# Output projection without a staged operand, TensorE's tiles written out, and zero rows stored early: one change to a one-core decoder step

## The reference, cut to what matters

```python
mixed = jnp.concatenate([y_rwkv, y_gmlp, y_sb], axis=-1) @ lw['w_out']
x = x + gate1 * mixed
h2 = rms_norm(x, lw['norm2_g']) * (1.0 + scale2) + shift2
moe = hier_moe(h2.reshape(B * T, D_MODEL), ...)   # top-1 group of 4, then top-2 of its 4 experts
x = x + gate2 * moe
```

## Time and profile before

| | us |
|---|---|
| median of 3 runs | 1441.96 |
| lowest and highest of the 3 | 1438.92, 1447.1 |
| the profiled execution, its own time | 1445.0 |
| its span, first to last instruction | 1443.4 |
| TensorE busy in the span | 1245.0 (86%) |
| VectorE, ScalarE, GpSimd busy | 594.9, 412.9, 174.6 |
| `out_project`, TensorE's first to last product | 912.1 to 1043.8 |
| `experts`, TensorE's first gate_up to its last matmul | 1098.7 to 1375.6 |
| `combine`, first matmul to the end | 1391.9 to 1443.4 |

### The profile page before, as it was taken

The page is one execution under the profiler, slowest core; times in us unless marked ns, Lnnn a source line. Parts: engine busy times, 40 slices in busy tenths (PEclk is TensorE's granted clock), DMA queues, the critical chain, the costliest instruction groups (busy, mean ns, idle before and its releaser), DMA issues. The chain is left out here.

```text
span 1443.4 us, 29072 instructions
## 1 busy us (share of the span) xinstructions
PE 1245.0 (86%) x10925; PEld 769.6 (53%) x10925; DVE 594.9 (41%) x1007; ACT 412.9 (29%) x850; POOL 174.6 (12%) x380
## 2 busy tenths in 40 slices
PE   5899989999976888999889987799926999999955
PEld 2465466565644565554569887344414555555421
DVE  3300514464555554466235556223371222222227
ACT  3100205565665563431112322012110111111113
POOL 0100101112121442000000000400001110011040
PEclk9899989999998899999989999799957999999978
DMA  9300305101000894247321000710107679856875
GB/s 359 115 0 0 112 15 161 41 5 46 17 1 17 309 404 129 71 138 258 91 104 18 4 4 3 219 70 30 44 8 287 208 251 349 294 164 231 296 264 179
DMA packets 88554, 191.78 MB, mean 133 GB/s; under 512 B 18523, under 2 KB 41570, under 8 KB 83203
## 3 DMA queue, kind: packets, MB, share of 16 engines
q1 hardware_dynamic: 70244, 142.36, 28.7%
q0 software_dynamic: 11056, 36.45, 7.2%
q10 hardware_dynamic: 7152, 11.55, 2.5%
HBM read 163.01 MB, written 27.31 MB: 132 GB/s over the span
## 5 line engine op out<-in xcount | busy, mean ns | idle before, releaser
L2660 PE MATMUL ex_ps_g<-all_mT,ex_xt 128*64 128x256 f32 x1344 | 156.2, 385 | 4.6 <-DMA all_mT<-in_exp_wu 3.2
L2270 PE MATMUL op_ps_o<-all_hT,op_m_t 128*128 128x512 f32 x256 | 115.7, 608 | 7.8 <-POOL op_m_t L2250 7.8
L2660 PEld LDWEIGHTS ex_ps_g<-all_mT,ex_xt 128*64 128x64 f32 x1344 | 93.7, 138 | 53.7 <-DMA all_mT<-in_exp_wu 4.8
L583 PE MATMUL rp_ps<-all_hT,kv_rp_w 128*128 128x384 f32 (+1 forms) x336 | 107.0, 473 | 0.8 <-PEq L1932 0.8
L352 PE MATMUL fr_big<-all_mT,all_hT 128*128 128x256 f32 (+3 forms) x288 | 95.7, 496 | 3.0 <-DVE all_hT L405 3.0
L1707 PE MATMUL at_ps_p<-all_hT,mix_at_w 128*128 128x363 f32 (+1 forms) x288 | 96.0, 476 | 0.0
L1862 DVE TENSOR_TENSOR_SCAN mix_v_g<-mix_v_g 128x1024 f32<-128x1024 f32 (+3 forms) x32 | 46.8, 1485 | 102.1 <-ACT at_A L1814 72.8
L583 PEld LDWEIGHTS rp_ps<-all_hT,kv_rp_w 128*128 128x128 f32 x336 | 62.5, 190 | 46.5 <-issue 10.9
L2679 PE MATMUL ex_ps_y<-all_hT,ex_hid_T 128*64 128x512 f32 x336 | 80.4, 599 | 4.3 <-DMA all_hT<-in_exp_wd 1.9
L2270 PEld LDWEIGHTS op_ps_o<-all_hT,op_m_t 128*128 128x128 f32 x256 | 48.5, 194 | 66.1 <-issue 57.9
L352 PEld LDWEIGHTS fr_big<-all_mT,all_hT 128*128 128x128 f32 (+1 forms) x288 | 54.6, 190 | 43.5 <-issue 38.2
(11 more groups left out here) (470 smaller groups left out, 2066.7 us busy)
## 6 DMA issues: line engine op xcount, KB each, us to landing
all_mT<-in_exp_wg SPq DMA_DIRECT2D x34, 512.0 KB, 5.8
all_mT<-in_exp_wu SPq DMA_DIRECT2D x34, 512.0 KB, 7.6
all_hT<-in_exp_wd SPq DMA_DIRECT2D x17, 1024.0 KB, 8.0
rp_w_mod<-in_w_mod SPq DMA_DIRECT2D x16, 1024.0 KB, 5.1
sa_v<-in_cache_v POOLq DMA_DIRECT2D x52, 256.0 KB, 5.6
slot_rows<-ex_y ACTq DMA_DIRECT2D x84, 128.0 KB, 5.9
rwkv_R<-in_cache_k SPq DMA_DIRECT2D x32, 256.0 KB, 5.7
rwkv_B<-in_cache_k SPq DMA_DIRECT2D x32, 256.0 KB, 6.1
```

Of the source, the lines that this page charges most:

```text
L583: last = nc.tensor.matmul(ps[:, i % SLOTS, 0:hi - lo], w[:, n % 2, k, :], hT[:, k, lo:hi], start=(k == 0), stop=(k == KT - 1))
L2270: last = nc.tensor.matmul(ps_o[0:m, u, lo:lo + 512], m_t[:, u, k, 0:m], w[:, k, lo:lo + 512], start=(k == 0), stop=(k == KT - 1))
L2660: final = nc.tensor.matmul(ps_g[rows, u, 0:DE], xt[:, k, HALVES[u]], w1[:, u, x_, k, :], start=(k == 0), stop=(k == KT - 1))
```

## The change

`m_t`, the semaphore `staged` and GpSimd's copies are gone; TensorE reads the tile out of `mT`. TensorE's loop over tiles 2 to 5 is written out. SP's zero loop moves from behind the last weight loads to behind `both(0)`, ahead of the loop of rounds.

```diff
@@ out_project
-        m_t = ph.sb("m_t", [P, 2, KT, P])
...
-                def stage(n, u, r):
-                    m = rows_of(n)
-                    pool.wait_ge(s["product_done"], n + 1)
-                    nc.gpsimd.tensor_copy(m_t[:, u, :, 0:m], mT[:, :, bass.ds(n * P, m)]).then_inc(s["staged"], 1)
-
-                each(pool, 2, stage)
                 for what, dst in ((2, gate), (4, gain), (3, shift)):
                     load_mod_sampled(pool, dst["s"], mod_rows, what, s["mod_s_loaded"])
-                with pool.Fori(1, NT // 2) as i:
-                    for u in range(2):
-                        stage(i * 2 + u, u, i)
-                stage(NT, NT % 2, NT // 2)
...
                     if half == 0:
-                        pe.wait_ge(s["staged"], n + 1)
                         pe.wait_ge(s["gated_done"], n + 1)
                     pe.wait_ge(w_loaded[half], 16)
                     for k in range(KT):
-                        last = nc.tensor.matmul(ps_o[0:m, u, lo:lo + 512], m_t[:, u, k, 0:m], w[:, k, lo:lo + 512],
+                        last = nc.tensor.matmul(ps_o[0:m, u, lo:lo + 512], mT[:, k, n * P:n * P + m], w[:, k, lo:lo + 512],
                                                 start=(k == 0), stop=(k == KT - 1))
...
-                both(0, 0, 0, first=True)
-                both(1, 1, 0)
-                with pe.Fori(1, (NT - 2) // 2) as i:
-                    both(i * 2, 0, i)
-                    both(i * 2 + 1, 1, i)
+                for n in range(NT - 2):
+                    both(n, n % 2, n // 2, first=(n == 0))
@@ experts, SP
                 load_w1(0, 0)
                 both(0)
-                rounds(sp, last, 1, both)
-                load_w1(1, last)
-                load_wd(0, last)
-                load_wd(1, last)
                 sp.wait_ge(zeros_ready, 1)
                 with sp.Fori(1, ROUNDS) as r:
                     with sp.If(r > last):
                         sp.dma_start(slot_rows[bass.ds(r * 2 * UNIT, 2 * UNIT), :], zeros[:, :]).then_inc(zeros_stored, 16)
                     with sp.Else():
                         sp.sem_inc(zeros_stored, 16)
+                rounds(sp, last, 1, both)
+                load_w1(1, last)
+                load_wd(0, last)
+                load_wd(1, last)
                 sp.wait_ge(zeros_stored, (ROUNDS - 1) * 16)
```

More of the change, by code:

```diff
@@ L2211, in out_project @@
         ps_r = ph.ps("ps_r", [P, 512])
-        names = ("gate_loaded mod_s_loaded r_loaded mod_loaded gains staged product_done gated_done x1_done sq_done ms_done rt_done rstd_done "
+        names = ("gate_loaded mod_s_loaded r_loaded mod_loaded gains product_done gated_done x1_done sq_done ms_done rt_done rstd_done "
                  "scaled h2_done turned ht_kept padded r_padded in_groups groups_kept routed logits_kept")
@@ L2281, in product_sampled @@
                             rows, at = slice(half * NS, half * NS + NS), slice(half * 512, half * 512 + 512)
-                            last = nc.tensor.matmul(ps_o[rows, u, at], m_t[:, u, k, 0:NS], w[:, k, at],
+                            last = nc.tensor.matmul(ps_o[rows, u, at], mT[:, k, n * P:n * P + NS], w[:, k, at],
                                                     start=(k == 0), stop=(k == KT - 1))
```

## The result

| | before | changed |
|---|---|---|
| median of 14 runs, us | 1447.87 | 1454.22 |
| lowest and highest, us | 1438.92, 1451.96 | 1447.45, 1460.93 |
| span of the profiled execution, us | 1443.4 | 1452.8 |

The ratio changed to before is 1.005, with a 95% interval of 1.0032 to 1.0068. On 1447.87 us that is 7.2 us more (4.6 to 9.8). (The two medians by themselves stand 6.35 us apart; the estimate of the ratio is a little larger, and its interval holds both.) The forecast was 7.5 more, at 1449.5 for a median of 1441.96; 1454.22 lies inside its range. The absolute time is no test of it, though: with 14 runs instead of 3 the median of the kernel before rose by 5.9 us.

What follows compares the result with a forecast made beforehand. TensorE, busy 86% of the span, was taken as the bound. 1445.0 - 2.1 - 5.1 + 14.7 = 1452.5 us for the profiled execution, which stands 3.0 above the median, so 1449.5 was forecast, range 1442 to 1457.

Steps and rivals of the forecast that it cites:

- Entry of the projection: Ahead of the projection's first product: without GpSimd's copy TensorE starts earlier, 2.1 us won.
- Rival 4: At the projection's first product: another wait just behind the copy removes the 2.1 us gain; 1451.6 us, chance 0.07.
- Copies and written-out tiles: In the projection's steady products: seven later copies and the written-out loop bring nothing, as TensorE has no idle time.
- End of the experts: Ahead of the combination: GpSimd's first gather no longer waits for zero stores, 5.1 us won, bounds 4.1 and 5.5.
- The first round: Ahead of the experts' fourth gate_up: SP's moved zero loop delays w1 pieces, 14.7 us lost, bounds 12 and 18.
- Not given back: In the experts' later rounds: TensorE is 97% busy, so all later work moves by the whole 14.7 us loss.
- second stall: At the next wd load's user in the experts: none expected, with 3 us to spare.
- Rival 2: In the experts' first round: 2 MB of zeros crowd the weights, stall 18 us or more; 1453 us, chance 0.15.
- The sum: Whole kernel: gains of 2.1 and 5.1 against a loss of 14.7, 7.5 us or 0.52% more.

Runs made afterwards that it cites:

- the projection's part: Kernel before with staged copies removed and tiles written out, zero loop left behind the last weight load; alone 1441.12 us, ratio 0.9976.
- four fixed stores without turns: Changed kernel with the early zero loop replaced by SP's fixed zero stores for rounds 21 to 24; 1443.4 us, ratio 0.9997.
- short loop at the early place: Changed kernel with the early zero loop starting at round 17, 4 turns that count and 4 that store; 1445.21 us, ratio 1.0009.
- early turns and late bytes: Changed kernel with the 24 early turns only counting and four zero stores issued behind the last weight load; 1449.54 us, ratio 1.002.

## Why the prediction was right, point by point

- **Entry of the projection**, 2.1 forecast: the idle time fell by 7.84 - 5.67 = 2.17 us, in every run with the projection's part (5.67 or 5.68 each time). The run of this part alone won 0.24%, or 3.5 us, with an interval that holds 2.1. Rival 4's other wait is there, the release of the output buffers (line 2370); it ends where TensorE's own step did, so it takes nothing of the 2.1. The two products behind it took 29.81 us where they took 30.34, but that is spread of the clock's rise: they took 29.69 to 30.61 in the nine executions without copies and 30.34 to 30.77 in the three with them. From the last matmuls of the phase before to the first turn the two kinds stand apart: 36.3 to 37.2 us without copies, 39.1 to 39.6 with them.
- **Copies and written-out tiles**, nothing forecast: no idle time in the steady stretch either way, and the written-out tiles alone at 1.0016 with 1 inside the interval. The rule of the Trainium skill (Runtime: NRT & Kernel Launch, Instruction fetch mechanics), that kernels prefer full unrolling because of fetches at taken branches, brought nothing in this case; no run here shows such a fetch.
- **End of the experts**, 5.1 forecast: 5.6, just above the bound of 5.5. The gather followed the landing of the last store by 0.3 us, not by the 0.8 taken over from the zero stores. (The landing of 2.3 us in the earlier trace rows is that of the two stores before the last two; in that trace ScalarE's own wait for the last one passed at 1379.5, 2.4 us behind its issue, so the reading holds.)
- **The first round**, 14.7 forecast: 15.26 and 15.46. By its parts: the gap 13.03 for 12.5, the slower gate_up behind it 2.16 for 2.2. The pieces left at 17.1 us more behind the wd load, not at 15.9, since the two register reads ahead of them took 0.88 and 0.90 us instead of 0.27 each; that was not in the sum. Piece 2 then landed in 4.8 us instead of 5.6, which took two thirds of it back.
- **Not given back**: the rounds from the disputed turn to the last down took 251.8 us where they took 253.5. The waits for weights in it sum to 2.2 us in the changed kernel and 5.1 before; but the run of the projection's part alone, which has no gap, shows 3.4 and the written-out tiles alone 1.3, and those two runs took 252.0 and 249.5 us for the stretch. So this is spread between executions and no recovery. No second stall came, as forecast: the next load of wd, issued at 1133.30, landed in 4.7 us, where the sum had 8.0.
- **Rival 2, crowding**: right in kind, small here. The four fixed stores without turns cost 7.64 us, and still 6.53 when SP's queue held none of them. The prediction argued from the 3.4 us landing of the zeros at the kernel's end, where no weights were being loaded; right behind the wd load they took 7.5 to 11.4. In the changed kernel the turns come first, so that the wd load has landed before the zeros leave, and they took 2.8 to 4.4. The prices don't add: 12.84 for the turns alone, 7.64 for the stores alone, 15.26 for both.
- **The sum**: 15.26 - 2.17 - 5.6 makes 7.5, the forecast to the tenth. That closeness is partly luck: the first round cost 0.6 more than forecast, and the end brought 0.5 more. The forecast sits on the bound of what can be told; it takes the 14 runs of each kernel to make the sign certain.

That tiles must be written out to be read in place was not tried the other way, with a loop that reads `mT` at a computed place. In the runs with fixed early stores the DMA engines show as full while the weights are late; whether the engines themselves or the memory that they write to sets that pace stays open.

## What to carry to other kernels

Before work is moved in an in-order queue to a place "where there is time", measure what it costs that queue, not what it moves: here 20 turns that store nothing held the queue for 11.6 us of the loop's 15.9, and the slack at the new place was 3.4. A move also brings the bytes beside other transfers: four stores that landed within 3.4 us each at the kernel's end took up to 11.4 beside a weight load. First ask whether the turns are needed: the known lower bound of a computed count removed 16 of them and gave nearly the whole gain of the end (0.9945 together with the projection's part) without a move. A queue that only grants permission ("already loaded") can stop the busiest engine as surely as one that moves data.

## What the runs showed of the hardware that was not expected

SP's register reads of one word in SBUF take 0.27 us (the median of 164 in the kernel before, which took 0.26 to 0.76). Right behind four zero stores in its own queue they take 0.81 to 0.96, up to 1.44 with the short loop at the early place, and 0.26 to 0.27 at the same place when the stores are left out there:

```profile
L2521 SPq TENSOR_LOAD <-all_expert x164: 262/269/763, 1084.1 to 1364.7; - x164
```
```profile
L2504 SPq TENSOR_LOAD <-all_expert x2: 878/887/896, 1123.1 to 1124.4; - x2
```
```profile
L2504 SPq TENSOR_LOAD <-all_expert x2: 262/268/274, 1118.5 to 1119.1; - x2
```

The first is the kernel before, the second the changed kernel, the third the run with early turns and late bytes. With the stores on ScalarE's queue they took 0.45 and 0.80, so stores of another queue slow them too. The Trainium skill (DMA: Bandwidth & Descriptors, Latency and other measured facts) gives `tensor_load` a floor of about 600 ns; the runs here show 0.26 us, and the measurement decides.
